# Keeping the first unit of query weights in two row pages: six pages for 78 slots, then eight

## The reference, cut to what matters

```python
q = (xt @ wq).reshape(128, 8, 2, 128)              # tokens in two tiles of 128, 8 heads
s = einsum('thcd,hckd->thck', q, sub_keys)         # 128 scores per half key
top_s, top_i = top_k(s, 16)
best_s, best_c = top_k(all 16 x 16 pair sums, 16)
expert = i1 * 128 + i2                             # one of 16384 experts
w = softmax(best_s)
act = gelu(einsum('thkd,td->thk', u[expert], xt))
out = einsum('thk,thkd->td', w * act, v[expert])
```

## Time and profile before

| | |
|---|---|
| median of the runs shown | 1106.22 us |
| the profiled execution's own time | 1105.7 us |
| its span | 1103.9 us |
| TensorE (PE) busy | 1014.6 us, 92% |
| VectorE (DVE) busy | 642.8 us, 58% |
| ScalarE (ACT) busy | 449.8 us, 41% |
| DMA, gathers | 269.89 MB, 59.1% of 16 engines' span |
| DMA, loads and stores issued by SyncE and plain copies | 76.95 MB, 18.3% |
| mean granted TensorE clock | 0.987 of full speed |

### The profile page before, as it was taken

One profiled execution on the slowest core, in us unless ns is written; L12 is line 12 of the kernel. 1 busy time (PEld: TensorE's weight loads), 2 busy tenths in 40 slices (PEclk: granted clock), 3 DMA queues, 4 the chain that ended last, 5 costly groups with the idle time before them and its releaser, 6 DMA issues.

```text
span 1103.9 us, 10619 instructions
## 1 busy us (share of the span) xinstructions
PE 1014.6 (92%) x3544; PEld 564.8 (51%) x3544; DVE 642.8 (58%) x1493; ACT 449.8 (41%) x1164; POOL 296.3 (27%) x305
## 2 busy tenths in 40 slices
PE   8999999999999998999989999878998877877878
PEld 8887458544686565555446555433443222222324
DVE  3515255305443479887747657557767767667443
ACT  1133244311354147466444345334445344344333
POOL 3000000001000024534534434334443443443420
PEclk9999999999999999999989999989999999999999
DMA  8435433244626359999999999999999999999990
GB/s 324 151 126 229 152 112 117 77 153 171 229 86 236 126 219 424 421 408 420 422 423 421 421 421 420 426 419 421 422 420 422 422 422 422 421 422 422 420 381 23
DMA packets 45591, 347.53 MB, mean 315 GB/s; under 512 B 4992, under 2 KB 6400, under 8 KB 8032
## 3 DMA queue, kind: packets, MB, share of 16 engines
q0 software_dynamic: 37296, 269.89, 59.1%
q1 hardware_dynamic: 8240, 76.95, 18.3%
HBM read 345.52 MB, written 1.05 MB: 314 GB/s over the span
## 4 chain that ended last, share of the span: by engine, by line
PE 60%; DMA 28%; ACT 5%; DVE 5%; issue 1%; POOL 0%; POOLq 0%; DVEq 0%
PE pp L1066 17%; DMA tail<-in_peer_uv,small 15%; DMA spare<-in_peer_uv,small 10%; PE pp L595 8%; PE pp L623 5%; PE pp L619 4%; PE pp L605 3%; PE pa L1025 3%; PE pp L750 3%; PE pp L770 2%; PE pp L728 2%; DMA ig<-in_peer_uv,small 2%; PE pp L960 2%; DVE tail L2212 1%; DMA kT<-in_peer_uv,small 1%; ACT diag L1518 1%
## 5 line engine op out<-in xcount | busy, mean ns | idle before, releaser
L1504 ACT ACTIVATE small<-small 128x1 f32<-128x1 f32 x256 | 51.6, 202 | 324.2 <-DVE small L2212 322.8
L1518 ACT ACTIVATE diag<-ident,small 128x128 f32<-128x128 f32 x256 | 102.8, 402 | 8.4
L595 PE MATMUL pp<-hT,ring 128*128 128x256 f32 x384 | 83.4, 379 | 0.8 <-DVE hT L1658 0.8
L1066 PE MATMUL pp<-xc_rg,diag 128*128 128x512 f32 x128 | 63.9, 623 | 17.0 <-ACT diag L1518 17.0
L1510 ACT ACTIVATE small<-small 128x1 f32<-128x1 f32 x256 | 75.3, 294 | 9.3
L1066 PE MATMUL pp<-kT,diag 128*128 128x512 f32 x128 | 65.4, 636 | 14.3 <-ACT diag L1518 14.3
L595 PEld LDWEIGHTS pp<-hT,ring 128*128 128x128 f32 x384 | 72.9, 190 | 10.8 <-issue 1.0
L1066 PE MATMUL pp<-spare,diag 128*128 128x512 f32 x128 | 65.4, 636 | 12.9 <-ACT diag L1518 12.9
L1066 PE MATMUL pp<-ig,diag 128*128 128x512 f32 x128 | 61.7, 605 | 9.9 <-ACT diag L1518 9.4
L1066 PE MATMUL pp<-sm,diag 128*128 128x512 f32 x128 | 61.8, 605 | 9.1 <-ACT diag L1518 9.1
L1066 PE MATMUL pp<-tail,diag 128*128 128x512 f32 x128 | 61.9, 606 | 8.8 <-ACT diag L1518 8.8
(11 more groups left out here) (477 smaller groups left out, 1878.7 us busy)
## 6 DMA issues: line engine op xcount, KB each, us to landing
ring<-in_wall SPq DMA_DIRECT2D x31, 2048.0 KB, 7.8
ring<-in_wall SPq DMA_DIRECT2D x4, 512.0 KB, 7.2
ring<-in_wall SPq DMA_DIRECT2D x2, 1024.0 KB
ring<-in_wall SPq DMA_DIRECT2D x1, 1280.0 KB
xs<-in_x SPq DMA_DIRECT2D x2, 512.0 KB, 3.8
post_g<-in_rows POOLq DMA_DIRECT2D x2, 512.0 KB, 8.2
tail<-in_wall SPq DMA_DIRECT2D x1, 1024.0 KB, 11.1
kT<-in_wall SPq DMA_DIRECT2D x1, 1024.0 KB, 13.1
```

The costliest lines, as they stand in the source:

```text
L595: ins = nc.tensor.matmul(buf[:, c, :], mine, h3[:, k, :], start=(k == 0), stop=(k == KC - 1))
L1066: ins = nc.tensor.matmul(acc[t][:, c, :], diag[:, n * P:(n + 1) * P], rows_uv[page_of(g)][:, D + c * HALF:D + (c + 1) * HALF], start=False ...
L1504: nc.scalar.activation(acts[:, at:at + BATCH], dots[:, at:at + BATCH], ACT.Gelu_apprx_tanh)\
L1518: nc.scalar.activation(diag[:, n * P:(n + 1) * P], ident[:, :], ACT.Copy, scale=wk[:, g % LAG:g % LAG + 1]).then_inc(s["diag_made"], 1)
```

## The change

The first unit of queries stays in its two pages until the second tile has used it too. The buffers `tail` and `kT` become the last two pages, and the first 78 slots use only the other six. From slot 78 on eight pages are used in turn; page 6 (`kT`) is first filled by slot 84 and page 7 (`tail`) by slot 85. The load of wq0b is left out. wq1b then follows `wp1` in ring slot 2, so it waits for `wp_used` 2 (after slot 54) and not for the use of wq0b (after slot 74). The waits of the first gathers follow the buffers to their new slots: the wait on `ao_full` moves from slot 7 to slot 2, that on `o_full` from slot 4 to slot 3, and that on `query_full` from slot 1 to slot 84, where it asks for part 5 of the queries.

```diff
-LATE_SLOT = {"wq0": RING, "wq1": 0, "wq2": 0, "wq3": 1, "wq0b": 2, "wq1b": 2, "ple": 0, "gw0": 1, "gw1": 2}
+LATE_SLOT = {"wq0": RING, "wq1": 0, "wq2": 0, "wq3": 1, "wq0b": RING, "wq1b": 2, "ple": 0, "gw0": 1, "gw1": 2}
...
 MANY = 8
+PAGES_FOR = [(78, 6)]
 
 
 def page_of(g):
+    for slots, pages in PAGES_FOR:
+        if g < slots:
+            return g % pages
+        g -= slots
     return g % MANY
...
-        rows_uv = [b[:, 0:2 * D] for b in (ig, kT, spare[:, 2 * D:4 * D], tail, rg, gl, ga, sm)]
+        rows_uv = [b[:, 0:2 * D] for b in (ig, spare[:, 2 * D:4 * D], sm, rg, gl, ga, kT, tail)]
...
+                if name == "wq0b":
+                    continue
...
-                if g == 1:
-
-                    pool.wait_ge(s["query_full"], 2)
-                if g == 4:
+                if g == 2:
+
+                    pool.wait_ge(s["ao_full"], 2)
+                if g == 3:
 
                     pool.wait_ge(s["o_full"], NT)
-                if g == 7:
-
-                    pool.wait_ge(s["ao_full"], 2)
+                if g == PAGE_SLOTS[6][0]:
+
+                    pool.wait_ge(s["query_full"], USED_BY["wq0b"])
...
-                at, to = 0, query_banks(n)[1]
-                if unit == "wq0":
-                    w, at = first_queries[n].rearrange("p (k n) -> p k n", k=KC), a
-                    pe.wait_ge(s[f"queries_kept{n}"], 16)
+                to = query_banks(n)[1]
+                if unit[:3] == "wq0":
+                    for half in range(a // (2 * P), b // (2 * P)):
+                        pe.wait_ge(s[f"queries_kept{half}"], 16)
+                    w = None
...
-                        mine = w[:, k, f - at:f - at + P]
+                        if w is None:
+                            mine = first_queries[f // (2 * P)][:, k * 2 * P + f % (2 * P):k * 2 * P + f % (2 * P) + P]
+                        else:
+                            mine = w[:, k, f:f + P]
```

## The result

The changed kernel takes 1112.9 us in the median of five runs (1112.14 to 1115.45) against 1106.22 before: a ratio of 1.0067, 95% interval 1.0056 to 1.0078. A repeat on another chip gave 1115.52 us (six runs, 1109.59 to 1118.14) against 1105.57: 1.0090 (1.0077 to 1.0103). So it is slower by 6.7 to 10 us, where 1.6 us were forecast; both medians lie above the range. The profiled execution took 1113.73 us, its span is 1112.0 us.

What follows compares the result with a forecast made beforehand. The DMA was taken to bound the second tile, DMA and TensorE at almost the same pace the first. -5.0 us of transfer and +6.6 us of DMA pauses gave +1.6 us: 1107.8 us, range 1103.9 to 1111.0.

Steps and rivals of the forecast that it cites:

- Bytes, -5.0 us: DMA transfers: dropping the 2 MB load of wq0b removes 5.0 us.
- Bare latency of a row, 5.5 us: Gathers into an idle DMA: a row lands 5.5 us after issue, ends 3.4 and 7.7; enters in three places.
- Row 10 goes out at 428.79 and lands at 434.3 ... 1.9 us behind: Start: row 10, landing at about 432.4 before, lands at 434.3 with six pages, so the DMA is 1.9 us behind.
- Rival (b): Slower: stretched gather issue, 1108.7 to 1109.7 us, or longer bare latency; 0.35 together with more TensorE loss around slots 53-57.
- the long issue: GpSimd's gather instruction taking 1.99 instead of 0.94 us; striking rows 34-36 or 66-69 adds 0.9 to 1.9 us.
- TensorE is 1.9 us late from slot 20: Slot 20 on TensorE: no slack there, so the start's 1.9 us passes on and does not grow by itself.
- Row 36, 3.0 us: Slots 20 to 56: row 36 lands at 507.7 instead of 502.75, 4.9 us behind; this stretch's term is 3.0 us.
- Rows up to 55 cost TensorE at most some 2 us more: Slots up to 55: with 4.3 us from landing to use, late rows cost TensorE at most some 2 us more.
- Rows 57 to 84, 1.7 us: Slots 57 to 84: row 69 lands 4.1 us behind, row 84 1.6 us behind; this stretch's term is 1.7 us.
- In the slots the DMA engines never pause: Kernel before, 470 to 1065 us: DMA share 1.01 at 416 to 421 GB/s, without a pause.
- The clock counted as nothing: TensorE's clock had no term in the sum; a possible fall was named only around slots 53 to 57, under slower.
- a bare latency of 6.4 us: Slower case: each gather taking 6.4 us in all three places gives +4.3 us, 1110.5 us.

Runs made afterwards that it cites:

- load_only: Kernel before with eight pages, without the load of wq0b (part 5 reads wq2's weights), wq1b right behind wq3: 1100.94 us, ratio 0.9955.
- start_six: As load_only, but with six pages for slots 0 to 23 and eight from slot 24: 1109.68 us, ratio 1.0031.
- mid_six: As load_only, but with six pages for slots 24 to 53, eight before and behind: 1105.59 us, ratio 0.9999.
- wait_eight: load_only with ScalarE held up between slots 19 and 20 by six copies to a tile nobody reads: 1102.61 us, ratio 0.9972.
- busy20: Changed kernel with three matmuls by a zero matrix put behind slot 19 on TensorE: 1113.5 us.
- early_six: Kernel before with its load of wq0b, six pages for slots 0 to 23 and eight from slot 24: 1114.65 us, ratio 1.0073.
- pages_only: Changed kernel with wq0b loaded again in the ring, six pages for 78 slots: 1116.60 us, ratio 1.0101.

## Why the prediction was wrong, step by step

- **Bytes, -5.0 us:** right (load_only -4.6).
- **Bare latency of a row, 5.5 us:** right for a row that meets an idle DMA (row 26: 5.6 us), and not for the three rows that I dated with it: row 10 took 11.4 us from issue to dot, row 36 7.2 and row 69 6.8. None of them had the DMA to itself: from issue to dot it moved 388, 379 and 382 GB/s, beside 207 for row 26. The Trainium skill, "DMA: Bandwidth & Descriptors", section "Anatomy of one DMA", gave 4.4 us as an estimate; row 26's 5.6 us, counted from the start of GpSimd's 0.94 us instruction to the dot, is 1.2 us longer, and the measurement decides.
- **"Row 10 goes out at 428.79 and lands at 434.3 ... 1.9 us behind":** the mis-sized term. The window 398 to 450 lost 3.3 us, and slots 13 to 19 got their rows 3.2 us late. I dated the whole start on one row with a bare latency. But the gathers of slots 6 to 10 go out 2.9 us apart on average, where a row costs the DMA 2.49, and it empties between them: from 422 to 424 us it moves 213 GB/s (before 422), from 430 to 434 311 and 336 (before 426 and 455), together 1.9 us of pause. Another 1.1 us lies from 410 to 412 (193 GB/s, before 438), behind row 3, which waited until 409.26. That wait is not the root of it, since start_six has row 3 on time and lost no less (7.5 us against 6.2). Row 10's issue itself took 2.00 us, as the earlier trace rows had shown for 428.79, and wq2's load, issued at 430.18, only 1.5 us behind it, was counted behind the row and not beside it; the dot of row 10 waits until 440.04. GpSimd's timeline of the changed kernel, and VectorE's dot of row 10:

```profile
417.19 0.94 POOL L559 DMA_INDIRECT ig<-in_peer_uv,small  x1 [3.33 <-PE pp L1078]
420.69 1.07 POOL L559 DMA_INDIRECT spare<-in_peer_uv,small  x1 [2.57 <-PE pp L1078]
422.91 0.94 POOL L559 DMA_INDIRECT sm<-in_peer_uv,small  x1 [1.15 <-PE pp L1078]
426.04 0.94 POOL L559 DMA_INDIRECT xc_rg<-in_peer_uv,small  x1 [2.20 <-PE pp L1078]
428.64 2.00 POOL L559 DMA_INDIRECT gl<-in_peer_uv,small  x1 [1.65 <-PE pp L1078]
...
440.04 1.23 DVE L2224 CUSTOM_DVE_ANT_0 gl<-gl,xc_rg 128x1024 f32<-128x1024 f32 x1 [4.07 <-DMA gl<-in_peer_uv,small]
```

  Rival (b) named the long issue, but for rows 34 to 36 and 66 to 69 only.
- **"TensorE is 1.9 us late from slot 20":** the step that failed. It was 3.2 us late, and then the clock took 3.0 more in that execution. I followed the wait of TensorE but not what it withholds: pages. Measured alone, the start costs 8.7 us, of which 1.7 is a fall of the clock at slot 20 in its profile (3.32 us instead of 1.98). My 1.9 ended at slot 20; the pause behind it (475 to 480 us at 154 GB/s, and 197 in the repeat without the fall) was in no term.
- **Row 36, 3.0 us:** low, though by how much is not separated. mid_six costs 4.7 us, but with its own step to six pages in it; there row 36 takes 6.9 us from issue to dot, 1.4 more than my 5.5. In the change the second window lost 7.3 us more than before, 4.3 in the execution without the clock's fall, the pause behind slot 20 included.
- **"Rows up to 55 cost TensorE at most some 2 us more":** wrong. Its slots end 6.2 us late up to slot 37, 7.9 at 39 and 9.9 at 54, where wq3's load stands before the row (13.0 us from issue to dot, 9.7 before).
- **Rows 57 to 84, 1.7 us:** low. 2.9 us more pause than before in the last two windows; 3.1 alone, 1.7 us of pause at its step included.
- **"In the slots the DMA engines never pause":** nearly, and that was the trap. Before the change 450 to 515 has 0.9 us of pause already, most of it from 490 to 495 us at 364 GB/s, where rows 33 and 34 reach their dots 8.6 and 7.9 us after their issue. So even with eight pages no queue was to spare there, and lateness at slot 20 had nowhere to go (wait_eight).

The mechanism was right in kind: with six pages rows go out too late to keep the DMA busy, and the pauses lie in the stretches that I named. But the three rows by which I dated them are not rows that met an idle DMA, and the pause that TensorE's own wait at slot 20 makes was in no term. The clock counted as nothing was wrong by 3 us in one of two profiles. Rival (b) had the sign. Of its two causes the long issue occurred at row 10 and not at rows 34 to 36 (0.94 us each) or 69 (0.95), and a bare latency of 6.4 us did not occur (5.6); its 1110.5 us were too low as well.

## What to carry to other kernels

When a buffer in flight is given up, price each place where the consumer stands still, with what that wait withholds from the producer, and follow it past the stretch in which it arises. A cyclic hand-out of buffers must change its length at a multiple of the old one. The spread grows too: on one chip the kernel before has executions within 2 us and the changed one within 9. That the lack of slack is the reason is not shown.

## What the runs showed of the hardware

The granted clock does not follow the idle time alone. Behind the same 2.99 us idle stretch of the same program slot 20 took 3.78 us in one execution and 1.98 in another; behind 1.90 us slot 7 took 3.68 us in busy20 and 1.98 in the repeat of the change. A fall cost 1.7 to 3 us. With eight pages the one at slot 7 stays hidden, since slot 20 waits for ScalarE anyway: load_only has it too (slot 7 takes 3.65 us, at 437.92), and its slot 20 starts at 472.08, 0.8 us later than in the kernel before and only 0.3 when both are counted from their first slot. A fall is not rare: behind 2.99 us of idle time at slot 20 early_six and start_six have it too (3.36 and 3.32 us), and pages_only, at 1.98 us, has not.
